# A two-block transformer on one core: scores ahead of the key turns, x loaded sooner, and a gated network entered by row tile

## The reference, cut to what matters

```python
# first block
mod = silu(c) @ w_ada + b_ada                      # shifts, scales and gates
h = modulate(rmsnorm(x, g_norm1), sh1, sc1)
cq, ckv, kpe, rq, rk, rv, rg = split_proj(h @ w_in)
k, v = mla_keys(ckv, kpe, g_kv, w_ukv, pos_grid)   # 8 heads, 96 wide
o_mla = latent_attention(q, k, v, k_c, v_c)        # 512 keys: 256 of x, 256 of the context
...
# second block, its end
y = cross_attention(rms_norm(h, g_x_pre), m, wq_x, wk_x, wv_x, wo_x)
h = h + rms_norm(y, g_x_post)
u = rms_norm(h, g_ffn_pre)
y = (silu(u @ w_gate) * (u @ w_up)) @ w_down
h = h + rms_norm(y, g_ffn_post)
```

## Time and profile before

| | us |
|---|---|
| median of 3 runs | 853.52 (853.22 to 854.45) |
| the profiled execution | 854.05 |
| its span, from the first to the last instruction | 852.2 |
| TensorE busy | 834.3 |
| VectorE busy | 588.2 |
| ScalarE busy | 468.1 |

### The profile page before, as it was taken

The page is one execution under the profiler, slowest core; times in us unless marked ns, Lnnn a source line. Parts: engine busy times, 40 slices in busy tenths (PEclk is TensorE's granted clock), DMA queues, the critical chain, the costliest instruction groups (busy, mean ns, idle before and its releaser), DMA issues. The chain is left out here.

```text
span 852.2 us, 12805 instructions
## 1 busy us (share of the span) xinstructions
PE 834.3 (98%) x4919; PEld 721.0 (85%) x4919; DVE 588.2 (69%) x917; ACT 468.1 (55%) x757; POOL 16.8 (2%) x24
## 2 busy tenths in 40 slices
PE   7999999999999999999999999999999999999997
PEld 5798888877899999987889977788977788888785
DVE  5885978787778777796767676577547655555444
ACT  6866364366366666563555684646545644444442
POOL 1001000000000000000000000010000000000000
PEclk9999999999999999999999999999999999999999
DMA  9973573165656666568758643244504666665541
GB/s 332 374 237 98 173 229 106 50 198 173 217 169 184 198 186 183 179 205 310 240 145 290 196 149 100 75 164 158 173 25 149 185 185 198 177 192 177 190 154 49
DMA packets 103667, 152.85 MB, mean 179 GB/s; under 512 B 6538, under 2 KB 55862, under 8 KB 103608
## 3 DMA queue, kind: packets, MB, share of 16 engines
q1 hardware_dynamic: 102296, 149.21, 54.5%
q10 hardware_dynamic: 1312, 2.83, 0.9%
HBM read 150.97 MB, written 1.05 MB: 178 GB/s over the span
## 5 line engine op out<-in xcount | busy, mean ns | idle before, releaser
L2087 DVE TENSOR_TENSOR w_lo<-raw,w_hi 128x1024 fp32r<-128x1024 f32 (+1 forms) x244 | 294.9, 1213 | 150.2 <-ACT w_hi L1521 149.4
L1521 ACT ACTIVATE w_hi<-raw 128x1024 fp32r<-128x1024 f32 (+1 forms) x244 | 254.5, 1050 | 201.2 <-PE bank L738 142.2
L736 PE MATMUL bank<-w_hi,hT_hi 128*128 128x512 f32 (+2 forms) x400 | 156.1, 390 | 1.3 <-DVE w_lo L2087 0.6
L738 PE MATMUL bank<-w_hi,hT_lo 128*128 128x512 f32 (+2 forms) x400 | 152.9, 382 | 0.0
L737 PE MATMUL bank<-w_lo,hT_hi 128*128 128x512 f32 (+2 forms) x400 | 152.6, 382 | 0.0
L839 PE MATMUL bank<-hT_hi,w_hi 128*128 128x256 f32 x512 | 145.0, 283 | 0.0
L840 PE MATMUL bank<-hT_lo,w_hi 128*128 128x256 f32 x512 | 144.9, 283 | 0.0
L841 PE MATMUL bank<-hT_hi,w_lo 128*128 128x256 f32 x512 | 144.9, 283 | 0.0
L840 PEld LDWEIGHTS bank<-hT_lo,w_hi 128*128 128x128 f32 x512 | 98.3, 192 | 0.0
L839 PEld LDWEIGHTS bank<-hT_hi,w_hi 128*128 128x128 f32 x512 | 98.3, 192 | 0.0
L841 PEld LDWEIGHTS bank<-hT_hi,w_lo 128*128 128x128 f32 x512 | 98.3, 192 | 0.0
(11 more groups left out here) (341 smaller groups left out, 1197.9 us busy)
## 6 DMA issues: line engine op xcount, KB each, us to landing
raw<-w_up_dram SPq DMA_DIRECT2D x132, 256.0 KB, 3.2
raw<-w_ada_dram SPq DMA_DIRECT2D x48, 512.0 KB, 4.7
raw<-w_down_dram SPq DMA_DIRECT2D x44, 512.0 KB, 4.1
raw<-w_in_dram SPq DMA_DIRECT2D x40, 512.0 KB, 4.6
raw<-w_gate_dram SPq DMA_DIRECT2D x44, 256.0 KB, 2.8
raw<-w_out_dram SPq DMA_DIRECT2D x16, 512.0 KB, 3.4
raw<-wk_x_dram SPq DMA_DIRECT2D x8, 512.0 KB, 4.7
raw<-wv_x_dram SPq DMA_DIRECT2D x8, 512.0 KB, 3.4
```

Source lines behind the costliest of these rows:

```text
L736: pe.matmul(o, xh, yh, start=first, stop=False, skip_group_check=skip)
L738: return pe.matmul(o, xl, yh, start=False, stop=last, skip_group_check=skip)
L1521: act.activation(unit_view(w_hi[n % NSPLIT], u), unit_view(raw[u % NRAW], u), ACT.Copy).then_inc(w_hi_ready, 1)
L2087: dve.tensor_tensor(unit_view(w_lo[n % NSPLIT], u), unit_view(raw[u % NRAW], u), unit_view(w_hi[n % NSPLIT], u).bitcast(F32), ALU.subtract ...
```

## The change

In the start, x's two row tiles are loaded after units 2 and 3 instead of 4 and 6. TensorE transposes x after units 4 and 5, then the vectors, and the fillers between the units of ada0 are 6, 12 and 10 (there were three behind each of six units). ScalarE and VectorE square and scale x earlier in their queues.

In the latent attention the second half's key turns, `turn_keys(1)`, come after the first two scores instead of before them, in banks 3, 0, 1 and 2. The copies of these keys are moved into the first rounds: on ScalarE behind the first exponential, on VectorE behind the second maximum, with one summed unit behind them (`more_sums(1)`); VectorE feeds no unit in round 0. A score of heads 4 to 7 waits for the second half's keys, the others no longer do. The eight fillers ahead of the scores go.

At the gated network, the last three units of "wo1" are worked by row tile. The first three units of "gu0" (`apart`) get buffers of their own, in memory that the recurrence, the cross attention's values and its keys no longer use, and are converted without waiting for slots. `res` is transposed by row tile and half (`turn_front(t, half)`, one bank each): (0, 0) ahead of row tile 1's last "wo1" unit, (0, 1) after "wo1", (1, 0) and (1, 1) between the units of "gu0" for row tile 0. The head of "gu0" runs its three units for row tile 0, then for row tile 1. The copies to `hT` become 128x128 each (`front`), in the order `FRONT_LO` on VectorE. The 14 and 8 fillers there go.

Left out below: the slots' dictionary in use, semaphores, the halves of edits that only follow from others, VectorE's `front(pieces)`, which is `hT_lo = PSUM * gain - hT_hi` on 128x128 pieces, and the calls that replace `turn("ffnpre")`.

```diff
@@ -272,8 +272,13 @@
     return LEAD["swa"] + sum(r < n for r in SWA_DENSE)
 
 
-BUSY = {"score": 8, "start": 17, "spread": 8, "ada": 3,  "ffnpre": 14, "gu0": 8}
-BY_ROW_TILE = ("wout2_1", "wo1", "dn1")
+BUSY = {"start": 17, "spread": 8, }
+BY_ROW_TILE = {"wout2_1": 2, "wo1": 3, "dn1": 2}
+
+
+HEAD = 3
+FRONT_HI = [(t, k) for t in range(T) for k in range(KD)]
+FRONT_LO = ([(0, k) for k in range(6)] + [(1, k) for k in range(6)] + [(0, 6), (0, 7), (1, 6), (1, 7)])
 
 
 def group_of(r):
...
@@ -312,6 +317,11 @@
 
     split_units = [u for u in range(len(units)) if not summed[u]]
     split_of = {u: n for n, u in enumerate(split_units)}
+    apart = units_of["gu0"][:HEAD]
+    ring = [u for u in split_units if u not in apart]
+    slot_of = {u: n % NSPLIT for n, u in enumerate(ring)}
+    slot_of.update({u: NSPLIT + n for n, u in enumerate(apart)})
+    slot_before = {u: ring[n - NSPLIT] for n, u in enumerate(ring) if n >= NSPLIT}
     ends = set(last_unit.values())
     inner = np.cumsum([u not in ends and not summed[u] for u in range(len(units))]).tolist()
 
...
@@ -747,21 +765,50 @@
                 for _ in range(n):
                     pe.transpose(o, ident, ident)
 
-            def panel(name, outs, step, before=None):
+            def front_ready(t, k):
+
+                if k % 4 == 3:
+                    emptied(pe, ("front", t, k // 4))
+                else:
+                    n = FRONT_LO.index((t, k)) + 1
+                    pe.wait_ge(front_lo, sum(x % 4 != 3 for _, x in FRONT_LO[:n]))
+
+            def panel(name, outs, step, before=None, between=None):
 
 
                 _, kind, kt, nk, cols, _ = next(x for x in panels if x[0] == name)
                 place[("end", name)] = place[outs[-1]]
                 keep_busy(ps(outs[0])[:, 0:P], BUSY.get(name, 0))
-                tail = units_of[name][-2:] if name in BY_ROW_TILE else []
+                tail = units_of[name][-BY_ROW_TILE[name]:] if name in BY_ROW_TILE else []
+                head = units_of[name][:HEAD] if name == "gu0" else []
                 for u in units_of[name]:
-                    if tail and u == tail[0]:
+                    if u in head[:-1]:
                         continue
-                    if tail and u == tail[1]:
-                        for v in tail:
-                            pe.wait_ge(unit_ready, v + 1)
+                    if head and u == head[-1]:
+                        for use in outs:
+                            for v in head:
+                                if use == outs[0]:
+                                    pe.wait_ge(unit_ready, v + 1)
+                                hi, lo = halves_of_unit(v, nk)
+                                for kk in range(nk):
+                                    k = units[v][1] + kk
+                                    front_ready(use[1], k)
+                                    ins = step(k, use, hi[:, kk, :], lo[:, kk, :], k == 0, False)
+                                if use == outs[-1]:
+                                    ins.then_inc(w_used, 1)
+                                else:
+                                    between(v)
+                        yield
+                        continue
+                    if u in tail[:-1]:
+                        continue
+                    if tail and u == tail[-1]:
                         for use in outs:
                             for v in tail:
+                                if use == outs[0]:
+                                    pe.wait_ge(unit_ready, v + 1)
+                                elif v == u and between is not None:
+                                    between(v)
                                 hi, lo = halves_of_unit(v, nk)
                                 for kk in range(nk):
                                     ins = step(units[v][1] + kk, use, hi[:, kk, :], lo[:, kk, :], False,
...
@@ -940,38 +989,32 @@
                     ins = pe.matmul(o[:, 2 * j:2 * j + 2], m[:, j * P:(j + 1) * P], sel_col, start=True, stop=True)
                 fill(ins, use)
 
-            for p in range(4):
+            for p in (0, 1, 3):
                 claim((f"ada{p}", 0), p)
             keep_busy(ps(("ada3", 0))[:, 0:P], BUSY["start"])
             pe.wait_ge(c_lo_ready, 2)
 
-            def chunk_unit(chunk):
-
+            chunk = ada_steps(0)
+            next(chunk)
+            for n in (6, 12, 10):
                 next(chunk)
-                keep_busy(ps(("ada3", 0))[:, 0:P], BUSY["ada"])
-
-            chunk = ada_steps(0)
-            for _ in range(4):
-                chunk_unit(chunk)
+                keep_busy(ps(("ada3", 0))[:, 0:P], n)
             run(chunk)
             chunk = ada_steps(1)
-            chunk_unit(chunk)
-            chunk_unit(chunk)
-            turn_vectors(1)
+            turn("x1", None, range(2))
             next(chunk)
+            turn("x1", None, range(2, 4))
+            turn_vectors(1, 2)
+            run(chunk)
             pe.wait_ge(in_sel, 16)
             ada_spread(0, 0)
-            run(chunk)
+            claim(("ada2", 0), 2)
             chunk = ada_steps(2)
             next(chunk)
-            next(chunk)
             ada_spread(1, 1)
-            next(chunk)
-            turn("x1", None, range(2))
             run(chunk)
             chunk = ada_steps(3)
             next(chunk)
-            turn("x1", None, range(2, 4))
             ada_spread(2, 2)
             run(chunk)
 
...
@@ -1091,9 +1134,8 @@
             retention(four[0:2])
             turn_keys(0, four[2:4] * 2)
             keys(1)
-            turn_keys(1, four[2:4] + four[0:2])
-
-            def attend(kind, work=()):
+
+            def attend(kind, work=(), between=None):
 
 
                 rounds = [r for r in ROUNDS if r[0] == kind]
...
@@ -1183,7 +1226,7 @@
                 yield
 
             wout0 = rows_steps("wout0", hT_hi, hT_lo, turn_before("o"), b=0)
-            attend("mla", mla_work())
+            attend("mla", mla_work(), lambda: turn_keys(1, (3, 0, 1, 2)))
             next(wout0)
 
             def mixed(kind, sem_):
...
@@ -1217,7 +1260,17 @@
                     sum_spread(10 + p)
                     run(steps)
 
-            def gated_rows(pre):
+            def turn_front(t, half):
+
+                use = ("front", t, half)
+                o = claim(use, next_small())
+                pe.wait_ge(res_ready, RES["xpost"] - 2 * T + 2 * t + half + 1)
+                for j in range(4):
+                    k = 4 * half + j
+                    ins = pe.transpose(o[:, j * P:(j + 1) * P], res[:, t, k * P:(k + 1) * P], ident)
+                fill(ins, use)
+
+            def gated_rows():
 
                 def turn_product(p):
                     use = ("product", p)
...
@@ -1230,9 +1283,15 @@
                             ins = pe.transpose(o[:, c:c + P], prod_row(p, t)[:, kk * P:(kk + 1) * P], ident)
                     fill(ins, use)
 
-                turn(pre)
+                turn_front(0, 1)
+
+                def second_tile(u):
+                    n = apart.index(u)
+                    if n:
+                        turn_front(1, n - 1)
+
                 for p in range(NFF):
-                    steps = rows_steps(f"gu{p}", hT_hi, hT_lo, None if p else turn_before(pre))
+                    steps = rows_steps(f"gu{p}", hT_hi, hT_lo, between=None if p else second_tile)
                     next(steps)
                     next(steps)
                     if p:
...
@@ -1516,9 +1575,11 @@
                         continue
                     n = split_of[u]
                     act.wait_ge(raw_landed[u % NRAW], landed[u])
-                    if n >= NSPLIT:
-                        released(act, split_units[n - NSPLIT])
-                    act.activation(unit_view(w_hi[n % NSPLIT], u), unit_view(raw[u % NRAW], u),
+                    if u in apart:
+                        ready(act, ("o",) + group_of(ROUNDS[-1])[0])
+                    elif u in slot_before:
+                        released(act, slot_before[u])
+                    act.activation(unit_view(w_hi[slot_of[u]], u), unit_view(raw[u % NRAW], u),
                                    ACT.Copy).then_inc(w_hi_ready, 1)
 
             def feed_one(stop=None):
...
@@ -1616,16 +1677,17 @@
                     ready(act, ("spread", ADA_ORDER[n - 2]))
                 free(act.activation(modrow[:, p % 2, :], ps(use)[:, :], ACT.Copy), use)
 
-            feed_units(6)
+            feed_units(3)
             act.wait_ge(in_x[0], 16)
             square("x1", 0, 0, res[:, 0, :])
-            ada(0)
-            feed_units(8)
+            feed_units(4)
             act.wait_ge(in_x[1], 16)
             square("x1", 0, 1, res[:, 1, :])
+            feed_units(5)
+            scale_row("x1", res[:, 1, :], row[:, 1, :])
+            feed_units(8)
+            ada(0)
             feed_units(10)
-            scale_row("x1", res[:, 1, :], row[:, 1, :])
-            feed_units(11)
             ada(1)
```

(63 more changed lines are left out.)

45 lines of the change are left out of this document (29 added, 16 removed).

## The result

The changed kernel takes 857.31 us (median of 6 runs, 855.20 to 859.23), the kernel before 853.38 us beside it (6 runs, 853.10 to 854.52): ratio 1.0043, interval 1.0033 to 1.0053. It is slower by 3.9 us, where I forecast 2.0 less. The profiled execution took 856.8 us.

The account below looks back on a forecast made before the run. The prediction took TensorE, busy 98% of the span, to bound the kernel. Gains of 1.2, 0.2 and 0.6 us, 2.0 in all, gave 852.05 profiled and a forecast of 851.5 us, range 849.0 to 855.0.

Parts of the forecast that it names:

- Part 1: Start: earlier x loads and transposes make "cq" start sooner; gain 1.2 us, bounds 0 and 1.8.
- The clock of 1.00 from 21 to 27: Start: listed sign that the forecast is right, the granted clock at 1.00 from 21 to 27 us.
- the sum: Whole kernel: gains of 1.2, 0.2 and 0.6 add to 2.0 us, taken from the profiled execution's 854.05.
- the added wait of 1.3 for unit 7's w_lo: Start: w_lo queued behind VectorE's copy of the vectors, starting at about 20.6 instead of 19.23; price 1.3 us.
- Part 2: Attention: two scores ahead of the second half's key turns; net gain 0.2 us, bounds 0 and 1.3.
- the idle that I had forecast: Attention: TensorE idle about 1.1 us ahead of the third turn of probabilities, at 174.7.
- Part 3: Gated network's front by row tile: "gu1" starts at 670.0 to 670.1 instead of 670.67; net gain 0.6 us.
- The stall: Front: first front transposes wait 2.0 us for the residual row, with no filler.
- its own of 850.2 to 852.8: Whole kernel: range in us of the main forecast alone, which was given 42%.
- The rival of the low clock: Front: clock stays low, price half the time at 1.2 GHz; two stretches (8 us) give 855.5; chance 13%.

Follow-up runs that it names:

- att_fill_5: Changed kernel with 5 dummy transposes ahead of attention's fifth score, nothing added at the front; 853.24 us, no falls in 11.
- att_fill: Changed kernel with 14 dummy transposes ahead of attention's fifth score, the front's idle left as it is; 852.83 us (ratio 0.9991).
- att_undone: Changed kernel with attention's old order put back, keeping the new start and front; 852.94 us, no falls in 11.
- before_no_fill: Kernel before the change without the 22 fillers (14 and 8) ahead of "gu0"; 853.99 us (ratio 1.0002).
- sums_later: Changed kernel with VectorE's second summed unit in attention moved a round back; 852.96 us, no falls in 11.
- gu0_banks: Changed kernel with "gu0" in the other pair of banks (2 and 3 in place of 0 and 1); 855.79 us (ratio 1.0016).
- front_undone: Changed kernel with the old front put back, keeping the new start and attention; 856.44 us (ratio 1.0030), falls in 9 of 12.
- conv_later: Changed kernel with VectorE's third conversion of "gu0" put behind the first residual row; 853.83 us (ratio 1.0009).
- front_mended: Changed kernel with VectorE's third "gu0" conversion behind the first residual row and "gu0" in the other banks, attention unchanged; median 855.07 us.

## Why the prediction was wrong, step by step

- **Part 1, −1.2: right in its size, partly by luck** (1.4 measured, 1.2 against executions of before at the full clock). The clock of 1.00 from 21 to 27 was named. But the sum was made against the profiled execution, whose clock had fallen, and against that one "cq" came 2.2 sooner: the added wait of 1.3 for unit 7's w_lo did not come (19.67, not 20.6). That error and the choice of the execution cancel but for some tenths. The low clock in the earlier trace rows lasted 3.4 us (2 x 0.15 x 3 + 2 x 0.42 x 3), where I wrote some 4.
- **Part 2, −0.2: the step that failed.** The queue of VectorE was right: third maximum at 170.55, key copies and two summed units ahead of it. Two things were not. "The first maximum led to its turn of probabilities in 1.83, so the third can be turned at 174.7" passes over the copy of the round before, which ScalarE has queued behind the third exponential and which frees the only bank: idle 1.66 in place of 1.1. And the idle was priced as a wait alone. The clock that falls behind it costs 4.5 in the median, which is more than the whole loss (857.31 to 852.83). With the idle that I had forecast, in att_fill_5, none of 11 executions fell. Without a fall part 2 is worth nothing: 852.83 with it (att_fill) and 852.94 without it (att_undone), and 75.9 against 75.7 us in the profiles.
- **Part 3, −0.6: wrong in sign by a missed term.** Without a fall it measures +0.8. The stall was 1.9 (2.0), four conversions took 1.14 us on ScalarE and 1.13 on VectorE (0.30 and 0.27 apiece forecast), and with the bank's wait taken away "gu1" follows the first front transposes in 15.60, where the forecast had 15.5 (654.55 to 670.05). What I missed is that "gu0" claims banks which VectorE empties only with times_gain of "wo1"'s second row tile: 1.4.
- **The sum without the clock**: the forecast of −1.2, −0.2 and −0.6 was 2.0 less; without falls all three together measure 0.5 less (att_fill, 852.83 against 853.33). The forecast of 851.5 would have been 1.3 too low: inside the whole range, just outside its own of 850.2 to 852.8. The rest is the clock.
- **The rival of the low clock** (13%, 855.5) had the mechanism and, within 2 us, the price, but at the front alone, for whose idle I had weighed it. Attention's idle I never asked about. The Trainium skill (TensorE: Matmul & The Clock Gate, Part 1: The HAM clock gate) says that the clock follows how busy TensorE has lately been, and that what watches this runs freely and isn't set back when a kernel starts. That part of the executions fall at one place and part don't agrees with it, and so does the start, where the clock fell in the profile of before and stood at 1.00 from 21 to 27 in that of before_no_fill, whose start is the same code.
- **Open**: the profile of the kernel after has a fall at the front as well, with an idle of 1.87 there; 44 executions of att_fill, att_fill_5, att_undone and sums_later have the same idle of 1.85 at the front, and all are at 0.998 or more. In the profile of gu0_banks attention fell and the front, with 1.85, did not, and in that of before_no_fill the front fell behind 1.41 and 1.11. So the length of one idle does not decide alone, and what does was not settled. That the single bank for turned probabilities stretches the idle is read from the code and the queue's order; a second bank was not tried.

## What to carry to other kernels

Price an idle stretch of a dense TensorE twice: as a wait, and as a fall of the clock behind it, which here made executions 1.5 to 9 us longer behind 1.66 us of idle at one place and none of them behind 1.15 at the same place; at the front 1.85 brought no fall in 44 executions. A few useless transposes ahead of the wait tell the two apart, as they bring no operand sooner. When a wait moves, follow its releaser's queue to the end (here a copy behind the exponential, and a bank emptied late), and look at the spread of the executions beside their mean clocks: two clusters say more than the median.

## What the runs showed of the hardware that I had not expected

- With an idle of 1.66 us in attention the mean clock was below 0.998 in 46 of 65 executions, and five of the six profiles show 1.2 GHz right behind it; with 1.15 us and less at that place it was so in none of 71.
- Once down, it stayed there for 3.4 us (after), 6.8 (front_undone) or some 10 (conv_later), though TensorE was busy for 3.00 of 3 in each window from 174 us on.
- The same kernel fell in some executions and not in others: front_mended 850.10 to 858.55 us in 12.
- 14 transposes of 128x128 whose results nobody reads kept the clock at its upper level (att_fill, no fall in 11).
- With x's transposes and the vectors ahead, TensorE was busy for 3.00 of 3 throughout 18 to 27, where I had expected one more wait.
